# Five norms between FFN, mixer and FFN: roots between GpSimd's pieces, last FFN tiles bank by bank, the first high part read straight from PSUM

## The chip, the cores and the metric

One core of one Trainium2 chip. The metric is the device time of one execution in microseconds (us); lower is better. TensorE multiplies, VectorE (DVE in the rows), ScalarE (ACT) and GpSimd (POOL) work on vectors, and SyncE's queue (SPq) issues the loads.

## What is computed

Two blocks one after the other on x of 256 tokens by 1024 features, all in float32. The first block has a parallel mixer (attention and retention), a cross-attention and a mixture of 32 experts. The second has two layers, each of this form:

```python
for l in range(DEPTH_2):
    x = _layer_norm(alpha * x + 0.5 * _swiglu(x, ffn_w_gu[l, 0], ffn_w_down[l, 0]), ln_g[l, 0], ln_b[l, 0])
    mix = _token_mixers(x, w_in[l], ...)
    x = _layer_norm(alpha * x + mix, ln_g[l, 1], ln_b[l, 1])
    x = _layer_norm(alpha * x + 0.5 * _swiglu(x, ffn_w_gu[l, 1], ffn_w_down[l, 1]), ln_g[l, 2], ln_b[l, 2])
```

`_swiglu(h)` is `(silu(h @ gate) * (h @ up)) @ down` with 2816 hidden features. `_layer_norm` subtracts the mean over the features, divides by the root of the variance, scales and shifts. `_token_mixers` projects x to 2208 columns, mixes the tokens in four ways and projects back.

## The kernel before, in words

Each engine runs one stream of instructions written out by hand, and semaphores order them between engines. Every matrix product is made of three: each float32 operand is split into a high part (rounded by writing it as fp32r) and a low part (the difference), and high x high, high x low and low x high are added in PSUM. ScalarE makes the weights' high parts (`act_high`, L512, and `ffn_high`, L928), VectorE or GpSimd the low ones (`low`, L521, and `ffn_low`, L933; GpSimd in four pieces of 512 columns).

An FFN (`pe_ffn`) goes over 22 tiles of 128 hidden features. `up` puts the gate and up columns of a tile into bank 4 or 5, ScalarE takes the silu (L1106), VectorE multiplies and splits the result (L1158 to L1162: `hf`, `hh`, `hl`), and `down` adds the tile's 1024 output columns for 256 tokens into banks 0 to 3 (tokens 0 to 127 in banks 0 and 1, the others in 2 and 3). `up` of a tile stands before `down` of the tile before it. After tile 21's `up` the last two tiles go bank by bank: tile 20 into banks 0, 1, 2 (nine products), then tile 21 into banks 0, 1, 2, with a semaphore (`f_bk`) behind each, then both into bank 3.

A norm then goes like this; there are six, here called norm 0 to norm 5, after FFN 0, the mixer and FFN 1 of layer 0, and the same of layer 1. `norm_sums` on VectorE adds each bank to x (L1188), takes its statistics (L1189), and after both banks of a token half joins them (L1192), negates the mean (L1194, first half alone) and writes the variance (L1196). GpSimd takes the root (`inverse_root`, L566). ScalarE multiplies mean and root (L1214) and scales the first half of x (L1215); VectorE scales the second half (L1208). TensorE (`pe_norm_T`) first runs 12 products of zeros (L1958), transposes the first half into banks 4 to 7 (L1010, eight), then runs four products of zeros (L1958, or L991 where they also clear banks 0 to 3) and transposes the second half. ScalarE applies gain and bias out of PSUM to `xf` (L1223, two row blocks of 128 features to a bank), VectorE casts that to the high part (`top`, L1235) and subtracts (`rest`, L1239). Before norms 0, 2 and 3 GpSimd has pieces to do: `low` of the projection's chunk 0 and 1 ahead of the roots of norms 0 and 3, `pool_second` (the second tile's low part, L939) ahead of the roots of norm 2. Its pieces for norms 1 and 4 come as late, and stay as they are.

After norms 1, 2 and 4 comes an FFN, whose first tile (`up_first`, L1050) takes all high row blocks first and the low ones after, gate columns (m = 0) before up columns (m = 1), into bank 4:

```python
for low_x in (False, True):
    for m in range(2):
        for k in range(KD):
            if m == 0 and k % 2 == 0: ...wait for the pair of row blocks...
```

After norms 0 and 3 comes the projection (`pe_part`, L1771) in nine chunks of weights, the first of them split in the same way. Between chunks VectorE does other work of the mixer: behind chunk 5's low part `squares()`, behind chunk 6's low part `scales()` (L1454 to L1466), which waits for a root of 16 columns from GpSimd.

In the first block TensorE issues the scores of the attention heads two at a time (`AHEAD1`, `pe_units`), between the retention's products (L2110).

Of the kernel before, what the change touches and what calls it, by code (L numbers as in the profile page):

```python
# [19 lines left out]
ALU = mybir.AluOpType  # L20
# [76 lines left out]
def build(nc, d_x, d_mem, d_w1, d_we, d_wf, d_w2, d_cT1, d_row1, d_wr, d_cT2, d_row2, d_ln, d_tab, d_bias, d_out):  # L97
    ctx = ExitStack()
    with ctx:
# [217 lines left out]
        xp_ok = sem("xp_ok")  # L317
        pre_ok = sem("pre_ok")
# [91 lines left out]
        AHEAD1 = {0: (0, 1), 1: (2, 3), 3: (4, 5), 5: (6, 7)}  # L410
# [103 lines left out]
        def low(eng, run, c, step=None):  # L514
# [4 lines left out]
            for c0 in range(0, n, step):  # L519
                part = slice(c0, c0 + step)  # L520
                ins = eng.tensor_tensor(slot_r[s][:, part], slot[s][:, part], run.highs[c % 2][:, part].bitcast(F32),  # L521
                                        ALU.subtract)
# [413 lines left out]
        def ffn_low_pieces(eng, t, p, done):  # L936

            for c0 in range(0, 2 * D, 512):
                ins = eng.tensor_tensor(wlu[p][:, c0:c0 + 512], ring[:, ring_tile(t) + c0:ring_tile(t) + c0 + 512],  # L939
                                        whu[p][:, c0:c0 + 512].bitcast(F32), ALU.subtract)  # L940
            ins.then_inc(done, 1)
# [21 lines left out]
        def pool_second(pool, g):  # L963
            pool.wait_ge(wl_ok, (g + 1) * FFN_W + 1)
            pool.wait_ge(wh_ok, g * FFN_W + 2)
            ffn_low_pieces(pool, 1, 1, pre_ok)
# [21 lines left out]

        def clear_sums(pe):
# [25 lines left out]
        def pe_ffn(pe, l, f):  # L1015
# [19 lines left out]
            def up_first():  # L1035

                pe.wait_ge(wl_ok, g * FFN_W + FFN_W + 1)
                if g == 0:
                    pe.wait_ge(t_out, tb + 1)
                for low_x in (False, True):  # L1040
                    for m in range(2):
                        for k in range(KD):
                            if m == 0 and k % 2 == 0:
                                if low_x:
                                    pe.wait_ge(t_out, tb + (k // 2 + 1))
                                else:
                                    pe.wait_ge(xh_ok, xb + (k // 2 + 1))
                            cols = slice(k * 2 * P + m * P, k * 2 * P + (m + 1) * P)
                            for w, v in (((whu, xl),) if low_x else ((whu, xh), (wlu, xh))):
                                ins = pe.matmul(bank[4][:, m * S:(m + 1) * S], w[0][:, cols], v[:, k],  # L1050
                                                start=(not low_x and m == 0 and k == 0 and w is whu), stop=False,
# [25 lines left out]
            with pe.Fori(0, FT // 2 - 1) as i:  # L1077
# [1688 lines left out]
```

## Time and profile before

| | |
|---|---|
| median of 3 runs | 1827.29 us (1823.26 to 1829.07) |
| the profiled execution, its own time | 1831.82 us |
| its span, first to last instruction | 1830.0 us |
| TensorE busy | 1645.0 us (90%), VectorE 853.7, ScalarE 639.8, GpSimd 262.6 |
| expert stage, loads at 407 to 427 GB/s | about 320 to 730 us |
| FFN 0, norm 0, mixer, norm 1, FFN 1, norm 2 | 731 to 1278 us |
| the same of layer 1, and norm 5 | 1278 to 1830 us |

TensorE's busy time counts matmuls that overlap, so 90% leaves idle time between stages only. In a tile of an FFN TensorE is never idle (one tile takes 8.55 us); what idle time there is in the second block stands at the norms, in the projection and among the mixer's heads.

### The profile page before, as it was taken

How to read it: one execution, taken by the hardware profiler on the slowest of the kernel's cores; microseconds unless marked ns; L12 is line 12 of the kernel's file. 1: busy time of each engine (PE TensorE's matmuls, PEld its weight loads, DVE VectorE, ACT ScalarE, POOL GpSimd, SP SyncE). 2: the span in 40 equal slices, each digit the busy share in tenths (PEclk: the TensorE clock that was granted, in tenths of full speed). 3: DMA queues.
4: the chain of work that ended last, by engine and by line, in shares of the span. 5: the costliest groups of instructions: out<-in, count | busy, mean ns of one | idle time of the engine just before them, and what ended most of it. 6: DMA issues, size and time to landing. Idle time of an engine off the chain costs nothing.

```text
span 1830.0 us, 29586 instructions
## 1 busy us (share of the span) xinstructions
PE 1645.0 (90%) x11837; PEld 1310.8 (72%) x11837; DVE 853.7 (47%) x1290; ACT 639.8 (35%) x948; POOL 262.6 (14%) x253
## 2 busy tenths in 40 slices
PE   8989999777766776999999899999999999899997
PEld 6777885333323332999977779998999977779996
DVE  4574443111110111555555655555655565666555
ACT  5445442100010011333433644444333333644442
POOL 1233210000000000100143422001300143431000
PEclk9989999977788887999999999999999999999999
DMA  9514578999999999945533054536454543055501
GB/s 393 171 38 138 195 283 334 425 426 427 426 426 426 425 426 407 358 176 188 198 138 138 24 198 180 185 124 236 176 194 180 187 149 124 24 207 182 196 35 46
DMA packets 60949, 421.38 MB, mean 230 GB/s; under 512 B 7008, under 2 KB 16064, under 8 KB 17216
## 3 DMA queue, kind: packets, MB, share of 16 engines
q1 hardware_dynamic: 59136, 409.13, 57.0%
q10 hardware_dynamic: 1728, 11.03, 1.7%
q8 instruction: 64, 1.05, 0.2%
q14 instruction: 21, 0.17, 0.0%
HBM read 419.08 MB, written 1.05 MB: 230 GB/s over the span
## 4 chain that ended last, share of the span: by engine, by line
PE 63%; DMA 10%; SPq 9%; DVE 5%; ACT 5%; POOL 4%; issue 4%; DVEq 0%; ACTq 0%; POOLq 0%
PE bank L1031 26%; PE bank L1072 12%; SPq L1683 9%; PE bank L1820 6%; PE bank L1771 5%; DMA ring<-in_we 4%; DMA more<-in_we 4%; PE bank L1846 2%; PE bank L650 2%; DMA ring<-in_wf 1%; PE bank L1984 1%; POOL small L566 1%; PE bank L1050 1%; PE bank L1965 1%; POOL wlu L939 1%
## 5 line engine op out<-in xcount | busy, mean ns | idle before, releaser
L1031 PE MATMUL bank<-xh,wlu 128*128 128x256 f32 x1344 | 379.9, 283 | 0.0
L1031 PE MATMUL bank<-xh,whu 128*128 128x256 f32 x1344 | 379.8, 283 | 0.0
L1031 PE MATMUL bank<-xl,whu 128*128 128x256 f32 x1344 | 379.8, 283 | 0.0
L1031 PEld LDWEIGHTS bank<-xh,whu 128*128 128x128 f32 x1344 | 257.0, 191 | 3.3
L1031 PEld LDWEIGHTS bank<-xl,whu 128*128 128x128 f32 x1344 | 256.9, 191 | 3.3
L1031 PEld LDWEIGHTS bank<-xh,wlu 128*128 128x128 f32 x1344 | 257.2, 191 | 0.0
L933 DVE TENSOR_TENSOR wlu<-ring,whu 128x2048 fp32r<-128x2048 f32 x84 | 196.3, 2337 | 51.2 <-ACT whu L928 51.2
L933 DVE TENSOR_TENSOR wld<-ring,whd 128x1024 fp32r<-128x1024 f32 x88 | 110.0, 1250 | 188.6 <-ACT whd L928 188.6
L928 ACT ACTIVATE whu<-ring 128x2048 fp32r (+1 forms) x88 | 167.2, 1902 | 3.5 <-DMA ring<-in_wf 3.5
L928 ACT ACTIVATE whd<-ring 128x1024 fp32r (+1 forms) x88 | 93.3, 1060 | 206.1 <-PE bank L1072 202.6
L650 PE MATMUL bank<-ring,xg 128*32 128x256 f32 x1424 | 104.0, 430 | 40.6 <-DMA ring<-in_we 40.6
L1820 PE MATMUL bank<-ring_r,xTh 128*128 128x512 f32 x384 | 112.9, 407 | 9.9 <-POOL ring_r L490 6.0
L1106 ACT ACTIVATE sg<-bank 128x256 f32<-128x256 f32 x88 | 33.8, 384 | 228.5 <-PE bank L1031 210.0
L939 POOL TENSOR_TENSOR wlu<-ring,whu 128x512 fp32r<-128x512 f32 x16 | 20.1, 1287 | 648.8 <-ACT whu L928 614.3
L650 PEld LDWEIGHTS bank<-ring,xg 128*32 128x32 f32 x1424 | 43.9, 119 | 96.1 <-DMA ring<-in_we 68.6
L669 PE MATMUL bank<-ring,hTe 128*32 128x256 f32 x832 | 75.6, 499 | 36.0 <-DMA ring<-in_we 27.6
L829 DVE TENSOR_TENSOR hmid<-hact,bank 128x128 f32<-128x128 f32 x32 | 9.2, 288 | 199.9 <-ACT hact L717 199.9
L1072 PE MATMUL bank<-whd,hl 128*128 128x512 f32 x320 | 100.9, 397 | 0.0
L1072 PE MATMUL bank<-whd,hh 128*128 128x512 f32 x320 | 100.5, 395 | 0.0
L1072 PE MATMUL bank<-wld,hh 128*128 128x512 f32 x320 | 100.4, 394 | 0.0
L1820 PEld LDWEIGHTS bank<-ring_r,xTh 128*128 128x128 f32 x384 | 73.5, 194 | 28.7 <-issue 8.8
L521 POOL TENSOR_TENSOR ring_r<-ring,high 128x512 fp32r<-128x512 f32 x32 | 41.3, 1322 | 349.2 <-ACT high L512 349.0
(317 smaller groups left out, 2745.6 us busy)
## 6 DMA issues: line engine op xcount, KB each, us to landing
ring<-in_we SPq DMA_DIRECT2D x141, 1024.0 KB, 26.8
ring<-in_wf SPq DMA_DIRECT2D x88, 1536.0 KB, 6.8
ring<-in_w SPq DMA_DIRECT2D x52, 1024.0 KB, 4.9
more<-in_we SPq DMA_DIRECT2D x51, 1024.0 KB, 25.7
ring<-in_w SPq DMA_DIRECT2D x32, 256.0 KB, 3.4
ln<-in_ln ACTq DMA_DIRECT2D x6, 1024.0 KB, 4.9
bias<-in_bias ACTq DMA_DIRECT2D x2, 2048.0 KB, 8.1
bias<-in_bias SPq DMA_DIRECT2D x1, 2048.0 KB, 20.1
```

Source lines behind the costliest of these rows:

```text
L521: ins = eng.tensor_tensor(slot_r[s][:, part], slot[s][:, part], run.highs[c % 2][:, part].bitcast(F32), ALU.subtract)
L650: ins = pe.matmul(bank[4 + e % 2][q * CAP:(q + 1) * CAP, 0:2 * P], xg[:, k, e * CAP:(e + 1) * CAP], w[:, kk, q], start=(k == 0), stop=(k = ...
L669: ins = pe.matmul(bank[6][q * CAP:(q + 1) * CAP, 0:2 * P], hTe[:, e % 2, k * CAP:(k + 1) * CAP], w[:, kk, q], start=(k == 0), stop=(k == 3 ...
L928: act.activation(dst[:], ring[:, bass.ds(ring_tile(t) + first, D if down else 2 * D)], ACT.Copy).then_inc(wh_ok, 1)
L933: eng.tensor_tensor(dst[:], ring[:, bass.ds(ring_tile(t) + first, D if down else 2 * D)], src[:].bitcast(F32), ALU.subtract).then_inc(done, 1)
L939: ins = eng.tensor_tensor(wlu[p][:, c0:c0 + 512], ring[:, ring_tile(t) + c0:ring_tile(t) + c0 + 512], whu[p][:, c0:c0 + 512].bitcast(F32), ...
L1031: ins = pe.matmul(bank[4 + p][:, m * S:(m + 1) * S], w[p][:, cols], v[:, k], start=(k == 0 and n == 0), stop=(k == KD - 1 and n == 2))
L1072: ins = pe.matmul(bank[2 * i + c][:], v[p][:, tok(i)], w[p][:, c * 512:(c + 1) * 512], start=False, stop=False, skip_group_check=True)
L1683: sp.dma_start(slot[s], src).then_inc(e_land[s], 16)
L1771: ins = pe.matmul(bank[sel + 2 * i + c0 // 512][:, 0:c1 - c0], v[:, k, tok(i)], w[:, kk, c0:c1], start=(k == 0 and m == 0), stop=(k == KD ...
L1820: ins = pe.matmul(bank[banks[2 * i + h]][:], v[:, k, tok(i)], w[:, kk, h * 512:(h + 1) * 512], start=(k == 0 and m == 0), stop=(k == KD - ...
L1846: ins = pe.matmul(bank[b][:, i * MD:(i + 1) * MD], v[:, k, tok(i)], w[:, k], start=(k == 0 and m == 0), stop=(k == KD - 1 and m == 2))
```

## The change

It has six parts. (1) Norms 0 and 3: the first root stands between the second and third piece of chunk 1's low part; norm 2: between the third and fourth piece of the second tile's. TensorE's second wait in `pe_norm_T` is for the variance, not the root, and the negation of the mean goes from VectorE to ScalarE. (2) The last FFN tiles: tile 20 goes into banks 0 and 1, then tile 21 into bank 0 (both products with `hh` first, that with `hl` last), then tile 20 into bank 2, and the rest as before. (3) The first pair of row blocks: VectorE makes the high part itself out of PSUM, one row block at a time with a semaphore each (`xk_ok`, `xh_ok`), and ScalarE takes that pair last (FFNs) or second (projection). (4) `up_first` goes row block by row block, gate and up columns together, into bank 3, which is cleared with one product of zeros ahead of tile 0's `down`; the low row blocks come in the order in which they are ready; the first pair of tiles is written out ahead of the loops. (5) `scales()` stands behind chunk 7's low part. (6) The heads' scores are issued one at a time from the third on.

```diff
-        AHEAD1 = {0: (0, 1), 1: (2, 3), 3: (4, 5), 5: (6, 7)}
+        AHEAD1 = {0: (0, 1), **{u: (u + 1,) for u in range(1, AH - 1)}}
...
+        ROWS_FIRST = (1, 2, 0, 3)
+
+        def gate_bank(t, p):
+
+            return bank[3 if isinstance(t, int) and t == 0 else 4 + p]
...
                     if i == 1 and b == 0:
-                        pe.wait_ge(pow_ok, POW1 + j // 3 * POW2 + (2, 6, 8)[j % 3])
+                        pe.wait_ge(var_ok, j // 3 * VAR2 + VAR1 + (2, 6, 8)[j % 3])
...
                 for low_x in (False, True):
-                    for m in range(2):
-                        for k in range(KD):
...
+                    order = ROWS_FIRST if low_x and g > 0 else range(4)
+                    for n, k in enumerate(2 * q + h for q in order for h in range(2)):
+                        if low_x and n % 2 == 0:
+                            pe.wait_ge(t_out, tb + (n // 2 + 1))
+                        elif not low_x and k == 0 and g > 0:
+                            pe.wait_ge(xk_ok, l * 3 + (0 if f == 0 else 2))
+                        elif not low_x and (k == 1 or k % 2 == 0):
+                            pe.wait_ge(xh_ok, xb + (k // 2 + 1))
+                        for m in range(2):
...
             up_first()
-            with pe.Fori(0, FT // 2 - 1) as i:
+            up(1, 1)
+            down_ready(0)
+            pe.matmul(bank[3][:], zeros[:, 0:P], zeros[:], start=True, stop=False, skip_group_check=True)
+            down(0, 0)
+            up(2, 0)
+            down(1, 1)
+            with pe.Fori(1, FT // 2 - 1) as i:
...
-            for b in range(3):
-                down_into(FT - 2, 0, b)
-            down_ready(FT - 1)
-            for b in range(3):
+            down_into(FT - 2, 0, 0)
+            down_into(FT - 2, 0, 1)
+            pe.wait_ge(wl_ok, (FT - 1) * 2 + (g * FFN_W + FFN_W + 2))
+            pe.wait_ge(f_hv, (FT - 1) * 2 + (g * FT * 2 + 2))
+            for w in (whd, wld):
+                pe.matmul(bank[0][:], hh[1][:, tok(0)], w[1][:, 0:512], start=False, stop=False, skip_group_check=True)
+            pe.wait_ge(f_h, FT - 1 + (g * FT + 1))
+            pe.matmul(bank[0][:], hl[1][:, tok(0)], whd[1][:, 0:512], start=False, stop=False, skip_group_check=True)\
+              .then_inc(f_bk, 1)
+            down_into(FT - 2, 0, 2)
+            for b in (1, 2):
                 down_into(FT - 1, 1, b, f_bk)
...
-                    if i == 0:
-                        st.then(dve.tensor_scalar(nmean, mean[:, 0, 0:1], -1.0, None, ALU.mult))
-                        st.sync()
...
         def act_norm(act, st, j):
 
+            act.wait_ge(var_ok, j // 3 * VAR2 + VAR1 + (1, 5, 7)[j % 3])
+            st.link(act.activation(nmean, mean[:, 0, 0:1], ACT.Copy, scale=-1.0))
             act.wait_ge(pow_ok, norm_pow(j))
...
+            def first_pair():
+                dve.wait_ge(t_ps, tb + 1)
+                for k, done in ((0, xk_ok), (1, xh_ok)):
+                    dve.tensor_scalar(high[:, k], bank[4][:, k * S:(k + 1) * S], gcol[:, j, 0, k:k + 1],
+                                      gcol[:, j, 1, k:k + 1], ALU.mult, ALU.add).then_inc(done, 1)
...
+            first_pair()
+            top(1)
             if paired:
-                for q in range(4):
+                rest(0)
+                rest(1)
+                for q in (2, 3):
                     top(q)
                     rest(q)
             else:
-                for q in range(4):
-                    top(q)
-                for q in range(4):
-                    rest(q)
+                rest(1)
+                top(2)
+                rest(2)
+                top(3)
+                rest(0)
+                rest(3)
...
-                    if c == 6:
+                    if c == 7:
                         scales()
...
+                low(pool, run2(l, 0), 0, 512)
+                low(pool, run2(l, 0), 1, 512, lambda c0: root(1, 0) if c0 == CH // 2 else None)
+                root(1, 1)
...
-                    pool_second(pool, g + 1)
-                for i in range(NT):
-                    pool.wait_ge(var_ok, l * VAR2 + (VAR1 + 7 + i))
-                    inverse_root(pool, rs[:, i:i + 1])
+                    pool_second(pool, g + 1, lambda c0: root(7, 0) if c0 == 3 * CH // 4 else None)
+                else:
+                    root(7, 0)
+                root(7, 1)
```

How the order of the instructions moves is seen in three places. GpSimd at norm 0: before, two chunks' pieces (`ring_r`) and then both roots (`small`):

```order
L521 TENSOR_TENSOR ring_r<-ring,high_0_88 128x512 [waits dh_ok]
L521 TENSOR_TENSOR ring_r<-ring,high_0_88 128x512 x3
L521 TENSOR_TENSOR ring_r<-ring,high_1_89 128x512 [waits dh_ok]
L521 TENSOR_TENSOR ring_r<-ring,high_1_89 128x512 x3
L566 TENSOR_TENSOR small<-small,minus_half 128x1 [waits var_ok] x2
```

and in the changed kernel:

```order
L524 TENSOR_TENSOR ring_r<-ring,high_0_88 128x512 [waits dh_ok]
L524 TENSOR_TENSOR ring_r<-ring,high_0_88 128x512 x3
L524 TENSOR_TENSOR ring_r<-ring,high_1_89 128x512 [waits dh_ok]
L524 TENSOR_TENSOR ring_r<-ring,high_1_89 128x512
L569 TENSOR_TENSOR small<-small,minus_half 128x1 [waits var_ok]
L524 TENSOR_TENSOR ring_r<-ring,high_1_89 128x512 x2
L569 TENSOR_TENSOR small<-small,minus_half 128x1 [waits var_ok]
```

The first root has moved ahead of two of the eight pieces. VectorE at norm 0, the tiles being the high part `xTh`, the full value `xf` and the low part `xl`; in the changed kernel this stands there, where before there were four pairs of CAST and TENSOR_TENSOR, one for each pair of row blocks in turn:

```order
L1269 TENSOR_SCALAR xTh_87<-bank,gcol 128x256 [waits t_ps]
L1269 TENSOR_SCALAR xTh_87<-bank,gcol 128x256
L1274 CAST xTh_87<-xf 128x512 [waits xf_ok]
L1280 TENSOR_TENSOR xl<-xf,xTh_87 128x512 [waits xh_ok,xf_ok]
L1280 TENSOR_TENSOR xl<-xf,xTh_87 128x512 [waits xh_ok]
L1274 CAST xTh_87<-xf 128x512 [waits xf_ok]
L1280 TENSOR_TENSOR xl<-xf,xTh_87 128x512 [waits xh_ok]
```

The first two instructions wait for TensorE's transposes alone, no longer for ScalarE. VectorE at the end of the projection, before; `ring_r` is a chunk's low part (6, 7 and 8 here), `proj` the scales:

```order
L521 TENSOR_TENSOR ring_r<-ring,high_0_88 128x2048 [waits dh_ok]
L1454 TENSOR_SCALAR proj_134<-proj_134,small 128x256 [waits pow_ok]
...
L1466 TENSOR_TENSOR proj_134<-proj_134,row_64 128x384 [waits dve_step] x2
L521 TENSOR_TENSOR ring_r<-ring,high_1_89 128x2048 [waits dh_ok]
L521 TENSOR_TENSOR ring_r<-ring,high_0_88 128x1280 [waits dh_ok]
```

In the changed kernel the scales stand between the last two, behind chunk 7:

```order
L1513 TENSOR_TENSOR proj_134<-proj_134,row_64 128x384 [waits dve_step] x2
L524 TENSOR_TENSOR ring_r<-ring,high_0_88 128x1280 [waits dh_ok]
```

So the wait for GpSimd's root (`pow_ok`) has moved behind chunk 7's low part and ahead of chunk 8's.

## Rows read from the trace of the kernel before

**Rows 1.** What TensorE waited for: us in total, times, longest

```profile
PE bank L1771 <- DVE ring_r L521: 4.5, 2, 2.3
```

**Rows 2.** Timeline around norm 0: start, us, engine, line, out<-in, count, idle before

```profile
920.96 5.00 POOL L521 TENSOR_TENSOR ring_r<-ring,high 128x512 fp32r<-128x512 f32 x4 [5.97 <-ACT high L512]
924.09 2.76 PE L1958 MATMUL bank<-zeros 128*128 128x512 bf16 x12
926.83 1.24 ACT L1215 ACTIVATE x<-x,small 128x1024 f32<-128x1024 f32 x1
927.82 0.15 DVE L1196 TENSOR_SCALAR small<-small 128x1 f32<-128x1 f32 x1
928.12 1.09 PE L1010 MATMUL bank<-ident,x 128*128 128x128 f32 x8 [1.26 <-ACT x L1215]
929.91 1.04 PE L1010 MATMUL bank<-ident,x 128*128 128x128 f32 x8
930.39 3.75 ACT L1223 ACTIVATE xf<-bank,gcol 128x256 f32<-128x256 f32 x8 [2.33 <-PE bank L1010]
931.93 0.73 PE L1771 MATMUL bank<-high,xTh 128*128 128x512 f32 x2 [0.98 <-DVE xTh L1235]
```

**Rows 3.** Timeline of the last tiles of FFN 1 and the start of norm 2

```profile
1266.17 0.39 PE L1057 MATMUL bank<-whd,hh 128*128 128x512 f32 x1
1267.57 0.43 DVE L1162 TENSOR_TENSOR hl<-hf,hh 128x256 fp32r<-128x256 f32 x1
1268.74 0.40 PE L1057 MATMUL bank<-wld,hh 128*128 128x512 f32 x1
1269.27 0.69 DVE L1188 SCALAR_TENSOR_TENSOR x<-x,bank 128x512 f32<-128x512 f32 x1 [1.28 <-PE bank L1057]
```

**Rows 4.** Timeline of norm 2, GpSimd, ScalarE and TensorE

```profile
1268.72 5.01 POOL L939 TENSOR_TENSOR wlu<-ring,whu 128x512 fp32r<-128x512 f32 x4 [160.57 <-ACT whu L928]
1271.98 1.06 ACT L928 ACTIVATE whd<-ring 128x1024 fp32r<-128x1024 f32 x1 [3.42 <-PE bank L1057]
1274.27 0.29 ACT L1214 ACTIVATE small<-small 128x1 f32<-128x1 f32 x1 [1.24 <-POOL small L566]
1275.89 1.09 PE L1010 MATMUL bank<-ident,x 128*128 128x128 f32 x8 [1.35 <-ACT x L1215]
```

**Rows 5.** Starts of FFN 1 and FFN 2: timeline of ScalarE and VectorE

```profile
1080.79 3.75 ACT L1223 ACTIVATE xf<-bank,gcol 128x256 f32<-128x256 f32 x8 [2.33 <-PE bank L1010]
1282.29 2.49 DVE L1239 TENSOR_TENSOR xl<-xf,xh 128x512 fp32r<-128x512 f32 x4
```

**Rows 6.** Chain of waits there: start, us, engine, tile, line, count

```profile
1085.06 4.58 PE bank L1050 x36
1281.52 6.75 PE bank L1050 x40
```

**Rows 7.** Timeline of the projection of layer 0

```profile
939.85 3.22 DVE L521 TENSOR_TENSOR ring_r<-ring,high 128x2048 fp32r<-128x2048 f32 x1 [3.67 <-ACT high L512]
965.88 1.92 ACT L512 ACTIVATE high<-ring 128x2048 fp32r<-128x2048 f32 x1 [3.66 <-PE bank L1771]
968.51 0.35 DVE L1454 TENSOR_SCALAR proj<-proj,small 128x256 f32<-128x256 f32 x1 [2.81 <-POOL small L566]
971.56 4.08 DVE L521 TENSOR_TENSOR ring_r<-ring,high 128x2048 fp32r<-128x2048 f32 x2
973.90 0.50 PE L1771 MATMUL bank<-high,xTh 128*128 128x512 f32 x1 [2.27 <-DVE ring_r L521]
```

**Rows 8.** TensorE in stretches: busy (count), granted clock, DMA share, GB/s

```profile
974.00:976.00 2.00, 2.00 (x7) 0.68 0.00 0
976.00:978.00 2.00, 2.00 (x6) 0.50 0.00 0
1282.00:1284.00 2.00, 2.00 (x10) 0.50 0.00 0
```

**Rows 9.** Timeline of VectorE among the first block's heads

```profile
110.39 0.69 DVE L2055 SCALAR_TENSOR_TENSOR lg<-bank,bias 128x512 f32<-128x512 f32 x1 [0.73 <-PE bank L1965]
```

More of the change, by code:

```diff
@@ L512, in act_high, with low @@
             act.activation(run.highs[c % 2][:, 0:n], slot[run.slots[c]][:, 0:n], ACT.Copy).then_inc(dh_ok, 1)
-        def low(eng, run, c, step=None):
+        def low(eng, run, c, step=None, between=None):
             eng.wait_ge(dh_ok, run.high + (c + 1))
@@ L1101, in act_ffn, with tiles @@
             else:
-                act_norm_T(act, l * 3 + (f - 1 if f == 0 else 1), tb)
+                act_norm_T(act, l * 3 + (f - 1 if f == 0 else 1), tb, (1, 2, 3, 0))
             def silu(t, p):
                 act.wait_ge(f_gu, t + (g * FT + 1))
-                act.activation(sg[:, p], bank[4 + p][:, 0:S], ACT.Silu).then_inc(f_sg, 1)
+                act.activation(sg[:, p], gate_bank(t, p)[:, 0:S], ACT.Silu).then_inc(f_sg, 1)
             def down_free(t):
                 act.wait_ge(f_dn, t + (g * (FT + 1) + 1))
-            with act.Fori(0, FT // 2 - 1) as i:
+            def tiles(i):
                 for p in range(2):
@@ L1117, in act_ffn @@
                     ffn_high(act, g, i * 2 + (p + 2), p, False)
+            tiles(0)
+            with act.Fori(1, FT // 2 - 1) as i:
+                tiles(i)
             j = l * 3 + 2 * f
@@ L1162, in hidden, with tiles @@
                 dve.tensor_tensor(hl[p][:], hf[:, p], hh[p][:].bitcast(F32), ALU.subtract).then_inc(f_h, 1)
-            with dve.Fori(0, FT // 2 - 1) as i:
+            def tiles(i):
                 for p in range(2):
@@ L1168, in dve_ffn @@
                     low(i * 2 + (p + 2), p, False)
+            tiles(0)
+            with dve.Fori(1, FT // 2 - 1) as i:
+                tiles(i)
             hidden(FT - 2, 0)
@@ L1215, in act_norm, with act_norm_T @@
             act.activation(x[:, 0], x[:, 0], ACT.Identity, bias=nmr, scale=rs[:, 0:1]).then_inc(x0_ok, 1)
[L1217 removed]
+        def act_norm_T(act, j, tb, order):
             act.wait_ge(gcol_ok, 1)
[L1220 to L1226 removed]
@@ L1228, in dve_norm_T @@
-        def dve_norm_T(dve, j, high, paired=False):
+            for q in order:
+                act.wait_ge(t_ps, tb + (q + 1))
+                if q == 0:
+                    act.wait_ge(xh_ok, j * 4 + 5)
+                for k in (2 * q, 2 * q + 1):
+                    ins = act.activation(xf[:, k], bank[4 + q][:, (k % 2) * S:(k % 2 + 1) * S], ACT.Identity,
+                                         bias=gcol[:, j, 1, k:k + 1], scale=gcol[:, j, 0, k:k + 1])
+                ins.then_inc(xf_ok, 1)
@@ L1577, in pool_layers, with root @@
                     pool_affine(pool, st, l * 3 - 1, (wl_ok, (g + 1) * FFN_W + 4))
-                for c in range(2):
-                    low(pool, run2(l, 0), c, 512)
-                for i in range(NT):
-                    pool.wait_ge(var_ok, l * VAR2 + (VAR1 + 1 + i))
+                def root(n, i):
+                    pool.wait_ge(var_ok, l * VAR2 + (VAR1 + n + i))
                     inverse_root(pool, rs[:, i:i + 1])
+                low(pool, run2(l, 0), 0, 512)
+                low(pool, run2(l, 0), 1, 512, lambda c0: root(1, 0) if c0 == CH // 2 else None)
+                root(1, 1)
                 pool_affine(pool, st, l * 3, (t_out, tb + 4))
@@ L1780, in pe_part @@
                         for kk in range(per):
+                            if kk == 1 and passes == (0, 1):
+                                pe.wait_ge(xh_ok, tops)
                             for i in range(NT):
```

47 lines of the change are left out of this document (20 added, 27 removed).

## The prediction

> **What bounds the kernel now.** I read the page first: TensorE is busy for nine tenths of the span, the other engines for half of it or less, and outside the expert stage, which this change does not touch, the loads keep up. So the second block's time is TensorE's, and the change can only win where TensorE idles or runs slowly. The list of its waits comes next [rows 1]: two waits of 2.3 us for a chunk's low part in the projection, one a layer. The rest stands around the norms, which I read in the timelines of norm 0 [rows 2], of the last tiles of FFN 1 [rows 3] and of norm 2 [rows 4]; the two halves of x are found there at the end of a chain sums, root, scaling, transposes, and TensorE waits for it. Behind a norm the FFN's first tile waits for VectorE's high parts [rows 5], and the chain of waits shows what it costs: the last 36 of its products take 4.58 us at full clock, but 40 take 6.75 us in FFN 2 [rows 6], where the granted clock stood at 0.50 [rows 8]. All sums below are made against the profiled execution, 1831.82 us by its own time; the median of the runs, 1827.29, is 4.5 us lower, and I take the same saving off it.
>
> **(a) Last tiles.** From the product at 1266.17 to the last at 1268.74 there are 11 steps of 0.233 us [rows 3]. Bank 0 was complete after 12 products, it now is after 9: 0.70 us earlier. Bank 1 stays at product 15, which holds the gain of VectorE's sums to 0.65, no more. The low part `hl`, ready at 1268.00 [rows 3], is wanted by the ninth product at about that time, so no stall comes in. The negation of the mean leaves VectorE, about 0.18 us with its step (an instruction of that size is 0.15, as L1196 in [rows 2]). Statistics come 0.83 us earlier. This counts in full only in norm 5, where nothing but the norm is left to do: **-0.8**. In norms 1 and 4 the roots come as before, so nothing changes there.
>
> **(b) Norms 0 and 3.** GpSimd works on the second of two chunks until 925.96, 920.96 + 5.00 [rows 2]; only then comes the root, and ScalarE scales from 926.83 to 928.07. Now the root stands before the last two of the four pieces, 2.5 us sooner, so after 923.46; the variance is there at 924.1 (by (a)), the root by 924.7, ScalarE is done about 926.3. That is earlier than TensorE is: its 12 products of zeros run from 924.09 for 2.6 us, to 926.7. So transposes begin at 926.7 for 928.12, **-1.4**, and the second half follows: four products of zeros end at 928.6 and the second half of x, whose root also stands 0.8 earlier, is ready by 928.3. The two pieces that moved behind the root feed chunk 1, wanted later than 927.2, when they end. Then the first pair: before, ScalarE starts `xf` at 930.39 and the first product runs at 931.93, 1.6 us after the transposes [rows 2]. Now VectorE writes one row block's high part straight from PSUM. No row of before shows this operation on 256 columns; from below half of the 512 columns out of PSUM (0.69, L1188 in [rows 3]) gives 0.35, from above all of it, 0.69; I take 0.43, what `hl` takes for 256 columns [rows 3], since the shape is the same. With 0.1 for the semaphore the first product comes 0.53 us behind the transposes for 1.6: **-1.07**. Together -2.5 a layer, **-5.0** (bounds -4.3 to -5.3). The work of the other pairs is the same, reordered; the low parts that start the third pass are 1.4 us earlier than wanted.
>
> **(c) The scales.** VectorE waits 2.81 us for GpSimd's root of 16 columns before it can start `scales` at 968.51, and then still has its work to do, so chunk 7's low part starts at 971.56 though its high part ended at 967.80 (965.88 + 1.92), and TensorE idles 2.27 us to 973.90 [rows 7]. Now VectorE starts it at 967.8. It takes about 2.35 (971.56 to 973.90), so it is there by 970.2, and TensorE wants it at 971.6: the stall goes, **-2.4 a layer, -4.9**. What is queued behind: the scales run from 970.2 to 973.3, chunk 8's low part (4.08 less 2.35, so 1.73) to 975.0, and TensorE, at 5.5 us a chunk (ScalarE's casts follow its chunks 3.66 + 1.92 = 5.6 apart, [rows 7]), wants it at 977.1. That leaves 2 us. The root itself is ready at 968.5 and no longer waited for.
>
> By [rows 7] another low part of 2048 columns took 3.22 us, while GpSimd was scaling; the 2.35 above had it idle. The Trainium skill ("SBUF — State Buffer", Who interferes with whom) says that VectorE and GpSimd share a port pair under an exclusive lock, the loser blocked for the whole instruction. This trace agrees in kind. By the page the worst is one GpSimd instruction, a piece of 1.25 us, met once by chunk 7 or the first pair; chunk 7 has a margin of 1.4, so the sum would be the same.
>
> **(d) The clock behind that stall.** Behind the idle stretch the granted clock is 0.68 and 0.50 for two stretches of 2 us [rows 8]. At full clock the same work would need 1.36 and 1.0: 1.6 us lost, and layer 1 shows the same. If the idle time goes, nothing lets the clock fall there; I take 1.5 each, **-3.0** (bounds 0 and -3.3).
>
> **(e) Starts of the FFNs behind norms 1, 2 and 4.** A is the time when ScalarE starts `xf`, 1080.79 in FFN 1 [rows 5]. The first tile ended at 1085.06 + 4.58 = 1089.64 [rows 6], A + 8.85, the last high pair having started at A + 4.27 with gate and up (m = 0, then all of m = 1) behind it. Now all eight products of a pair come together, and only eight of the high pass are left for the last pair. ScalarE leaves out the first pair, so the last pair is cast one pair sooner (two times 0.47 of 3.75 / 8), at A + 2.8 for its input, A + 3.9 with the cast and what stands on VectorE before it, a low part of 0.62 (2.49 / 4) [rows 5]. Eight products at 0.127 (4.58 / 36) to A + 4.9, sixteen low ones to A + 6.9: **-2.0 each, -6.1**. VectorE has about 0.2 us to spare here before tile 1; if it hasn't, each gives 1.0 only (-3).
>
> **(f) Norm 2.** GpSimd's four pieces take 5.01 us from 1268.72 [rows 4]; the root now comes after three, at 1272.5. But ScalarE casts `whd` to 1273.04 first, then has the negation (as L1214, 0.29), product and scaling to do (1.24): x is ready at 1274.9 where transposes began at 1275.89, **-1.0**.
>
> **(g)** The FFN 2 start: 40 products in 6.75 us would take 5.1 at the pitch of FFN 1; 36 against 36, 1.3 us come from the clock [rows 6, 8]. With less idle time ahead it should not fall: **-1.3** (bounds 0 and -1.6).
>
> **(h)** One product of zeros more an FFN, 0.22 (2.76 / 12, [rows 2]), four times: **+0.9**. In FFN 0 nothing is gained, for its operands are ready early.
>
> **(i) The heads.** From the third on scores come one at a time, so fewer of them stand ahead of VectorE's first logits, for which it waited 0.73 [rows 9]: **-0.8** (bounds -1.5 and +1, if a single score ahead is too little and VectorE waits among the heads).
>
> Sum: -0.8 - 5.0 - 4.9 - 3.0 - 6.1 - 1.0 - 1.3 + 0.9 - 0.8 = -22.0. The profiled time would be 1809.8, the median **1805** (1827.29 - 22.0 = 1805.3).
>
> **The rivals.** *Clock* (0.19): (d) and (g), 4.3 us, come not from the idle time but fall elsewhere, and as many again may be found: 1809.6 to 1813.9. For it speaks that 0.50 is granted after some stalls and not after others. The Trainium skill ("TensorE: Matmul & The Clock Gate", Part 1) has a gate that follows recent activity on a grid of its own, so that a dip can shift in time as work shifts; the sum by it would hold the 4.3 us back, 1809.6. The dips I read stand only behind idle stretches [rows 8], which is why I hold to the sum.
>
> *The stall moves* (0.08): the root of 16 columns or the scales are late, chunk 8 waits as chunk 7 did: (c) and (d) lost, 7.9 us, 1813. It decides if scales end over 2 us later than reckoned.
>
> *The feed* (inside the range): FFN starts give 1.0 each and no more, 1808.5.
>
> *Little happens* (0.04): the chain at the norms has another link, as the products of zeros behind the norms or VectorE's casts, and each gain waits there: above 1822.
>
> *Slower* (0.03): the first pair of tiles is written out ahead of the loop in each FFN on three engines, so TensorE's stream grows by some hundreds of instructions, which must be fetched. If fetching them stalled TensorE by over 22.0 / 4 = 5.5 us an FFN, the sum turns: at 7 us an FFN the time is 1805.3 + 28 = 1833. Against it: the 36 products of [rows 6] are written out as well and run at 0.127 without a gap.
>
> **How the numbers follow.** The sum as it stands has 0.66. Its own bounds (b 0.7, e 3, i 1.8 up; 1.0 or so down, and a stronger gain in dips elsewhere, 4) give about 1799 to 1810; with the clock rival the range goes up to 1814, and down to 1797, beyond which less than 2 in 10 is left. A measurement can tell 0.3%, 5.5 us. Faster by more than that: 0.66 + 0.19 + 0.08 less a remainder, 0.92; same 0.05; slower 0.03.
>
> **What would show it.** In the changed kernel's profile: the wait of 2.3 us for `ring_r` absent from TensorE's waits, the clock at 1.00 behind it; chunk 8 without a wait; the transposes of norm 0 about 1.4 us earlier after the last product, set by the products of zeros; VectorE's first high part about 0.43 us; FFN 1's first tile ending about 6.9 us after its transposes; the last bank sums of the end 0.8 us nearer to the last product. Wrong is the prediction if TensorE's idle time has shrunk and the time hasn't (the clock), or if a first tile's end is at A + 8 or more (VectorE).

## The result, and the profile after

The changed kernel's median is **1806.27 us** (12 runs, 1800.8 to 1821.08), that of the kernel before 1827.72 (12 runs, 1821.37 to 1832.12): ratio 0.9887, 95% interval 0.9869 to 0.9904, so 1.0 to 1.3% faster. The forecast was 1805.

The page of the changed kernel, against a span of 1830.0 and TensorE at 1645.0 us before:

```profile
span 1805.4 us, 29475 instructions
PE 1645.2 (91%) x11841; PEld 1305.3 (72%) x11841; DVE 856.1 (47%) x1289; ACT 617.6 (34%) x935; POOL 258.8 (14%) x253
```

TensorE is as long busy as before: what went is time in which it waited. Its waits between 930 and 1060 us (us in total, times, longest), the stretch that holds the projection and the mixer of layer 0:

```profile
PE bank L2035 <- ACT xT L2091: 4.1, 7, 0.8
PE bank L2026 <- ACT lg L2085: 1.4, 4, 0.5
```

The wait for `ring_r` of [rows 1] is absent, as is its clock stretch [rows 8] at that place. The projection's end in the timeline (start, us, engine, line, out<-in, count, idle before):

```profile
958.76 1.92 ACT L513 ACTIVATE high<-ring 128x2048 fp32r<-128x2048 f32 x1 [3.66 <-PE bank L1820]
960.72 2.29 DVE L524 TENSOR_TENSOR ring_r<-ring,high 128x2048 fp32r<-128x2048 f32 x1 [2.12 <-ACT high L513]
962.92 0.35 DVE L1501 TENSOR_SCALAR proj<-proj,small 128x256 f32<-128x256 f32 x1
965.97 1.49 DVE L524 TENSOR_TENSOR ring_r<-ring,high 128x1280 fp32r<-128x1280 f32 x1
```

Chunk 7's low part now starts 0.04 after its high part; before it was 3.8 later [rows 7]. The scales find their root ready and end at 965.9, and chunk 8's low part at 967.5 keeps nobody waiting.

Norm 0 in the timeline, to be read beside [rows 2]:

```profile
919.51 2.76 PE L2009 MATMUL bank<-zeros 128*128 128x512 bf16 x12
919.52 0.56 POOL L569 TENSOR_TENSOR small<-small,minus_half 128x1 f32<-128x1 f32 x1 [0.83 <-DVE small L1226]
920.50 1.24 ACT L1247 ACTIVATE x<-x,small 128x1024 f32<-128x1024 f32 x1
922.11 1.04 PE L1021 MATMUL bank<-ident,x 128*128 128x128 f32 x8
924.27 0.99 DVE L1269 TENSOR_SCALAR xTh<-bank,gcol 128x256 fp32r<-128x256 f32 x2
924.55 1.93 ACT L1257 ACTIVATE xf<-bank,gcol 128x256 f32<-128x256 f32 x4 [2.81 <-PE bank L1021]
924.87 0.73 PE L1820 MATMUL bank<-high,xTh 128*128 128x512 f32 x2
```

The root stands at 919.5, in front of two of GpSimd's pieces; ScalarE is done at 921.74, 0.37 ahead of the transposes, which start as the products of zeros end (twelve at 0.22 behind 919.51). VectorE's high part of one row block out of PSUM takes 0.50 (0.99 for two), and the first product comes 0.60 behind VectorE's start.

The first tiles of FFN 1 and FFN 2, in the chain of waits (start, us, engine, tile, line, count), to be read beside [rows 6]:

```profile
1070.22 6.39 PE bank L1061 x48
1265.06 6.39 PE bank L1061 x48
```

In both FFNs the 48 products follow each other at 0.13. Before, FFN 2's last 40 alone took 6.75.

The new order of the last tiles has a price of its own. The last product of tile 20 into bank 1 and the first ones of tile 21 into bank 0, at the end of FFN 0:

```profile
914.87 0.40 PE L1069 MATMUL bank<-wld,hh 128*128 128x512 f32 x1
915.22 0.47 PE L1106 MATMUL bank<-whd,hh 128*128 128x512 f32 x1
915.52 0.40 PE L1106 MATMUL bank<-wld,hh 128*128 128x512 f32 x1
```

The steps are 0.35 and 0.30 where all others are 0.23. So from the last `hl` to the last product of an FFN it is 4.17 us for 3.97 before, in all four FFNs, and 3.97 again in the run with the old order (experiment 8): the order costs 0.2 an FFN. Why the two steps are longer is not shown.

**A ledger by stretches.** The starts of single instructions serve as marks in every profile: the first silu of each FFN, and ScalarE's casts of the chunks of weights (a stretch "FFN" ends at the cast of the next projection's chunk 0, a stretch "rest of the projection, mixer" at the last cast before the next FFN). How much shorter a stretch is than in the first profile of before (its length there in brackets) tells what each part did, however the whole run fell out. The last two columns are the same programs, profiled once more in the runs `after_again` and `before_again` below.

| stretch | changed | changed, again | before, again |
|---|---|---|---|
| start to first silu of FFN 0 (742.00) | -5.01 | -6.75 | -4.52 |
| FFN 0 (165.3) | +0.23 | +0.23 | +0.01 |
| norm 0, to cast of chunk 2 (30.64) | -2.28 | -2.29 | 0.00 |
| rest of the projection, mixer, layer 0 (126.91) | -4.21 | -6.95 | +0.03 |
| norm 1, start of FFN 1 (24.87) | -1.77 | -1.79 | +0.02 |
| FFN 1, norm 2, start of FFN 2 (198.62) | -3.76 | -3.76 | -0.09 |
| norm 3 (30.62) | -2.27 | -2.27 | 0.00 |
| rest of the projection, mixer, layer 1 (126.90) | -3.55 | -3.60 | +0.05 |
| norm 4, start of FFN 3 (24.87) | -1.79 | -1.79 | +0.02 |
| norm 5, last `hl` to the first scaling of x (8.04) | -0.70 | -0.71 | 0.00 |

FFNs 2 and 3 give +0.2 each, as FFN 0. Every stretch repeats within 0.1 us, but for the first block and the two with a mixer.

What the clock takes is reckoned in all that follows as (one less the granted clock) times the time. From the cast of chunk 8 to the end of a mixer's stretch the kernel before loses 5.1 us a layer in this way, in all six mixers seen (its two profiles and that of `heads_alone`, whose second block is the same): 1.7 behind the stall [rows 8], and 3.4 at the mixer's end. That second dip was not among the rows of before. Here it is in layer 0 (length, TensorE's busy time and count, granted clock, DMA share, GB/s):

```profile
1046.00:1048.00 2.00, 1.41 (x9) 0.60 0.03 8
1048.00:1050.00 2.00, 2.00 (x12) 0.50 0.94 291
1050.00:1052.00 2.00, 2.00 (x9) 0.50 0.57 238
1052.00:1054.00 2.00, 2.00 (x8) 0.69 0.00 0
```

### The profile page after: what moved, and what is told of

Read it like the earlier page. It is cut to its first block, busy times and chain, and to the rows that moved or that the text cites. A ratio compares the mean times of both kernels' runs of the same rounds, so it can differ in the third digit from the quotient of the medians.

```text
span 1805.4 us, 29475 instructions
## 1 busy us (share of the span) xinstructions
PE 1645.2 (91%) x11841; PEld 1305.3 (72%) x11841; DVE 856.1 (47%) x1289; ACT 617.6 (34%) x935; POOL 258.8 (14%) x253
## 4 chain that ended last, share of the span: by engine, by line
PE 66%; DMA 11%; SPq 10%; issue 4%; ACT 3%; DVE 3%; POOL 3%; DVEq 0%; ACTq 0%; POOLq 0%
PE bank L1042 27%; PE bank L1084 12%; SPq L1732 10%; DMA ring<-in_we 9%; PE bank L1820 7%; PE bank L1871 6%; PE bank L1897 2%; DMA ring<-in_wf 1%; PE bank L2035 1%; PE bank L1061 1%; PE bank L653 1%; PE bank L2016 1%; PE bank L2009 1%; PE bank L1069 1%; POOL ring_r L491 1%
## 5 line engine op out<-in xcount | busy, mean ns | idle before, releaser
L931 ACT ACTIVATE whd<-ring 128x1024 fp32r (+1 forms) x88 | 93.2, 1060 | 206.8 <-PE bank L1084 203.2
L653 PE MATMUL bank<-ring,xg 128*32 128x256 f32 x1424 | 111.7, 454 | 37.8 <-DMA ring<-in_we 37.8
```

What stands on the lines that cost most here:

```text
L653: ins = pe.matmul(bank[4 + e % 2][q * CAP:(q + 1) * CAP, 0:2 * P], xg[:, k, e * CAP:(e + 1) * CAP], w[:, kk, q], start=(k == 0), stop=(k = ...
L931: act.activation(dst[:], ring[:, bass.ds(ring_tile(t) + first, D if down else 2 * D)], ACT.Copy).then_inc(wh_ok, 1)
```

## The experiments

There are twelve runs: the changed kernel and the one before once more each, and ten kernels that differ from one of the two. Where a kernel ran several times, its median stands beside that of before, taken at the same time.

**1. The changed kernel once more** (`after_again`).

> The changed kernel once more, for one more profile. If the ledger of stages is a property of the program, the stages of the second block repeat within 0.3 us each: norm 0 -2.3, projection with what follows it -4.1, FFN 1 start -1.8, norm 2 with FFN 2 start -3.8 against the first profile of before. If instead the granted clock falls by chance, the stretches at 0.5 and 0.7 stand elsewhere and the stages differ by 1 to 3 us. The first block's gain of 5.8 us, of which I had forecast 0.8, should be seen in either case; if it shrinks to about 1, it was chance.

1802.55 us (one run). The ledger above: norms and FFN starts repeat to 0.02 us. The mixer of layer 0 does not: it is 2.7 us shorter, where the first profile had the clock at 0.50 to 0.70 from 1034 to 1042 us, at the end of the heads and behind it, and this one at 1.00.

**2. The scales behind chunk 6 again** (`scales_behind_6`).

```diff
-                    if c == 7:
+                    if c == 6:
                         scales()
```

> The change with the scales back behind chunk 6's low part, nothing else undone. My theory (c and d together): TensorE waits 2.3 us for ring_r in each layer, and the clock is at 0.5 to 0.7 behind it; in all 3.9 a layer, so 7.8 us slower than the changed kernel, 1814. Rival: the clock has nothing to do with that stall; then 4.9 slower, 1811, and the granted clock is 1.00 behind the stall or falls in other stretches.

1813.75 us (6 runs, before 1829.28; ratio 0.9927, 0.9906 to 0.9948), 7.5 above the changed kernel where the theory said 7.8 and the rival 4.9. The intervals of the two ratios leave some 2 to 12 us for this difference, so the medians don't choose between the two. The stall is back in both layers, but the clock behind it is not the same in both. The timeline's row of the stall in layer 0, then TensorE's stretches (length, busy and count, granted clock, DMA share, GB/s), two behind that stall and three behind that of layer 1:

```profile
965.81 0.50 PE L1820 MATMUL bank<-high,xTh 128*128 128x512 f32 x1 [2.28 <-DVE ring_r L524]
```

```profile
966.00:968.00 2.00, 2.00 (x9) 1.00 0.00 0
968.00:970.00 2.00, 2.00 (x10) 1.00 0.00 0
1503.00:1505.00 2.00, 1.72 (x6) 0.84 0.00 0
1505.00:1507.00 2.00, 2.00 (x6) 0.50 0.00 0
1507.00:1509.00 2.00, 2.00 (x9) 0.81 0.03 8
```

The same stall, and in layer 0 no dip behind it. So the fall to 0.50 is not a fixed price of the stall, though close to it: it stands behind seven of the eight such stalls in the profiles, and in none of the 20 mixers without the stall is there a fall at that place. Stretch of the mixer in the ledger: -1.53 and +0.54, for -3.55 to -6.95 in the changed kernel.

**3. The scales moved, nothing else** (`scales_behind_7_alone`, on the kernel before).

> The kernel before with only the scales moved behind chunk 7's low part. Theory: the stall of 2.3 us and the clock stretch behind it go, 3.9 a layer in the ledger from chunk 8's cast to the mixer's end, 7.8 in all, 1821 for 1828.5. Against it: the seven profiles with the stall gone show stretches at granted clock 0.50 among the heads that cost 0, 0, 0.5, 1.1, 2.0, 3.4 and twice 8.0 us by execution, so the median may give 2 to 3 us less (1824) and the runs spread wider than before's.

1820.15 us (6 runs, 1815.45 to 1823.8; before 1829.23; ratio 0.995, 0.9932 to 0.9968), 9.1 less by the medians. In the ledger -2.70 and -2.68 in the mixers, where 2.3 is the stall: in this profile the clock takes 5.1 us a layer from the cast of chunk 8 on, as much as in before; the fall behind the stall is gone, and another one has come in among the last heads.

This run shows something else. FFN 1, norm 2 and the start of FFN 2 are 1.25 shorter here, though none of their instructions were changed: the granted clock, 0.50 at FFN 2's start in the three profiles of before and `heads_alone` [rows 8], is 1.00 there in this one. That is the whole of (g), without any idle time taken away.

**4. The heads of the first block** (`heads_in_pairs` on the changed kernel, `heads_alone` on the kernel before).

```diff
-        AHEAD1 = {0: (0, 1), **{u: (u + 1,) for u in range(1, AH - 1)}}
+        AHEAD1 = {0: (0, 1), 1: (2, 3), 3: (4, 5), 5: (6, 7)}
```

> The change with the first block's scores two at a time again, nothing else undone. By my forecast 0.8 us slower, 1807. By the trace of the changed kernel, where the heads end 3.5 us earlier and the first block 5.8 us earlier, 3 to 6 us slower, about 1811, with a stretch at granted clock 0.5 among the heads (110 to 150 us) as in before.

> The kernel before with only the first block's scores one at a time. By my forecast 0.8 us faster than before; by the trace of the changed kernel 3 to 6 us faster, 1822 to 1824, with TensorE's granted clock at 1.00 from 110 to 150 us. If it is no faster, the first block's gain belongs to where the work fell, not to this part.

In pairs on the changed kernel: 1810.68 us (6 runs; before 1829.28; ratio 0.9909, 0.9886 to 0.9932), 4.4 above, with overlapping intervals. Alone on before: 1826.51 (12 runs; ratio 0.9988, 0.9972 to 1.0004), no difference that can be told. The profiles say more: from the first score to the end of the heads it takes 42.3 to 42.9 us singly (eight profiles), 44.8, 45.0, 45.0 and 46.5 in pairs (four), and 49.7 and 51.5 singly in the other two (experiments 8 and 9). Most of that is clock, which takes 1.7 us there in each of the eight, 3.4 to 5.1 in the pairs, and 10.2 and 12.0 in the two; what is left is 40.6 to 41.2 in the eight and 39.7 to 41.6 in pairs. In those two the clock falls and stays. Stretches of `last_tiles_as_before`, whose first block is the changed kernel's:

```profile
104.00:110.00 6.00, 6.00 (x21) 0.50 0.00 0
110.00:120.00 10.00, 10.00 (x39) 0.50 0.01 2
120.00:130.00 10.00, 9.54 (x60) 0.92 0.00 0
```

**5. The kernel before once more** (`before_again`).

> The kernel before once more, for a second profile. The ledger of the changed kernel's two profiles and of the one with the heads in pairs starts the second block 4.5 to 6.7 us earlier than the first profile of before, though the pairs have the first block of before word for word. My theory now: the first profile of before lost about 4 us there to stretches of a lower granted clock, by chance; so this one starts its second block 3 to 5 us earlier than that one (first tile of FFN 0 done at 737 to 739 for 742.0), and its stages behind that repeat within 0.3 us, but for one stretch among the heads of a layer. Rival: before is slow there for a reason in the program, and repeats 742.0 within 1.

1827.31 us. Its first silu comes 4.52 us earlier, everything behind it in step within 0.1 us a stretch. So the profiled execution of before was slow by 4.5 us in its first block alone, of which 1.5 lay between the first score and the end of the heads; that is the whole distance of its time to the median. Counted from this second profile, the single scores bring FFN 0's first silu 0.5 to 3.3 us earlier in eight profiles, and 3.1 and 9.9 later in the two above.

**6. The roots behind the pieces again** (`roots_behind_pieces`).

```diff
-                low(pool, run2(l, 0), 1, 512, lambda c0: root(1, 0) if c0 == CH // 2 else None)
+                low(pool, run2(l, 0), 1, 512, None)
+                root(1, 0)
...
-                    pool_second(pool, g + 1, lambda c0: root(7, 0) if c0 == 3 * CH // 4 else None)
+                    pool_second(pool, g + 1, None)
+                    root(7, 0)
```

> The change with both roots behind GpSimd's pieces again (norms 0, 2 and 3). Theory: the transposes of norms 0 and 3 wait for the scaled x as before, 1.4 us each, and norm 2 gives 1.0 back: 3.8 us in all; in the ledger norm 0 gains 0.9 for 2.3 and norm 2 with its FFN start 2.8 for 3.8. Rival: VectorE's statistics and the products of zeros set the end, and the roots' place gives under 0.5 each.

1817.28 us (one run). Norm 0 gains 0.94 for 2.28, norm 3 0.91 for 2.27, norm 2 with its start 2.77 for 3.76: 3.7 us, as expected. ScalarE waits for the root again, and TensorE for ScalarE:

```profile
921.17 1.24 ACT L1247 ACTIVATE x<-x,small 128x1024 f32<-128x1024 f32 x1
922.46 1.09 PE L1021 MATMUL bank<-ident,x 128*128 128x128 f32 x8 [1.13 <-ACT x L1247]
```

The other 7 us of this run lie in the mixers, -2.41 and +2.05, with the clock at 0.50 for 10 us on end in layer 1 and twice more behind that (7.8 us lost to the end of the heads).

**7. The first pair through `xf`, and gate before up** (`first_pair_through_xf`, `gate_before_up`). The first lets ScalarE take the pairs in order and VectorE cast:

```diff
-            for q in order:
+            for q in range(4):
                 act.wait_ge(t_ps, tb + (q + 1))
...
-                dve.wait_ge(t_ps, tb + 1)
+                dve.wait_ge(xf_ok, j * 4 + 1)
                 for k, done in ((0, xk_ok), (1, xh_ok)):
-                    dve.tensor_scalar(high[:, k], bank[4][:, k * S:(k + 1) * S], gcol[:, j, 0, k:k + 1],
-                                      gcol[:, j, 1, k:k + 1], ALU.mult, ALU.add).then_inc(done, 1)
+                    dve.tensor_copy(high[:, k], xf[:, k]).then_inc(done, 1)
```

The second puts `for m in range(2)` of `up_first` outside the row blocks, the waits on m == 0.

> The change with the first pair's high part made from xf again (ScalarE takes the pairs in order 0 to 3, VectorE casts row block by row block). Theory: the projection starts 1.1 us later behind norms 0 and 3 (ledger 1.2 for 2.3), and the FFNs' last pair comes 0.5 to 0.6 later behind norms 1, 2 and 4 (1.2 for 1.8): 3.8 us in all. Rival: TensorE is held by the last pair's high part in the projection too, and the first pair's start is worth under 0.5.

> The change with the first tile's gate products ahead of its up products again, within the high and the low pass. Theory: 36 products instead of 24 are left behind the last pair's high part, 12 more at 0.12: the first tile of FFNs 1, 2 and 3 ends 1.4 us later, 4.3 us in all (ledger 0.4 for 1.8). Rival: the feed of low parts holds the end, and it gives under 0.7 each.

1812.3 and 1812.27 us (one run each). The first pair: norms 0 and 3 gain 1.43 and 1.40, so it is worth 0.85 and 0.87 there; FFN starts 1.06, 3.05 and 1.03, so 0.7 each; 3.9 in all. Gate before up: FFN starts 0.33, 2.35 and 0.36, so 1.4 each, 4.3 in all. Both sums are as expected to 0.1 us; of the first the parts are less so, for the projection's start was put at 1.1 and the FFN's at 0.5 to 0.6. In the first of them the clock fell in the mixer of layer 0 and stayed down for 10 us while TensorE's records leave no gap. Just before, it had waited 0.78 for ScalarE:

```profile
1003.57 1.08 PE L2032 MATMUL bank<-proj,xT 128*128 128x64 f32 x8 [0.78 <-ACT xT L2088]
```

```profile
1004.00:1006.00 2.00, 1.96 (x17) 1.00 0.00 0
1006.00:1008.00 2.00, 2.00 (x12) 0.51 0.00 0
1008.00:1010.00 2.00, 2.00 (x11) 0.50 0.00 0
1010.00:1012.00 2.00, 2.00 (x11) 0.50 0.02 4
```

**8. The last tiles in their old order** (`last_tiles_as_before`).

```diff
+            for b in range(3):
+                down_into(FT - 2, 0, b)
+            down_ready(FT - 1)
+            for b in range(3):
+                down_into(FT - 1, 1, b, f_bk)
```

These lines stand in place of the changed kernel's.

> The change with the last two tiles' products in the order of before (tile 20 into banks 0, 1, 2, then tile 21), nothing else undone. Theory: bank 0 is complete 0.7 us later, so the statistics start later and norm 5 takes 0.65 more; norms 0 and 3 lose less, for the products of zeros set their end (x was ready 0.3 before they ended), about 0.3 each; norm 2 loses 0 to 0.5. In all 1.3 to 1.8. Rival: all of the 0.7 in norm 5 came from the removed negation, and the order gives nothing.

1816.28 us (one run, with the long clock stretch of the first block shown above). Norm 5 gives 0.20 for 0.70, so the order is worth 0.50 and the negation, by subtraction, 0.20; norms 0 and 3 lose 0.48 and 0.50, norm 2 0.1 or less: 1.5 in all. I had 0.3 for norms 0 and 3. In norm 0 the first half's transposes come 0.36 later behind FFN 0's last product, for x is no longer ready before the products of zeros end; the second half's come 0.25 later still and the first product of the projection another 0.05; and the last product itself comes 0.2 earlier, the price of the new order given back.

**9. Single scores in the second block too** (`mixer_scores_singly`).

```diff
+        AHEAD2 = {0: (0, 1), **{u: (u + 1,) for u in range(1, 19)}}
```

> The change with the second block's scores one head at a time too (from the third on), as the change does in the first block. Theory: TensorE's waits of 0.3 to 0.8 us for ScalarE at every second head are filled by the scores that now come there, the heads end 2 to 4 us a layer earlier, and with less idle time the granted clock falls there less often: 1798 to 1802, and a narrower spread. Rival: the chain softmax, transpose, copy of one head sets the pitch, whatever TensorE does between; then the same within 2 us, or slower by up to 4 where a score is late for VectorE.

1812.74 us (5 runs, 1811.78 to 1825.89; before 1829.23; ratio 0.9913, 0.9895 to 0.993): slower than the change by 6.5 by the medians, by 4.8 by the ratios, whose intervals just touch. Faster it is not, and the ledger is clearer than the runs. Two heads' scores of `after_again`, then one head's of this kernel:

```profile
992.42 1.13 PE L2016 MATMUL bank<-qkT 32*128 32x256 f32 x8
```

```profile
995.62 1.12 PE L2015 MATMUL bank<-qkT 32*128 32x256 f32 x4
```

Eight products for two heads take what four take for one, for two heads lie in different rows of the array. The Trainium skill ("TensorE: Matmul & The Clock Gate", Part 3: Packing small matmuls) says that products in different row groups run at the same time; these rows agree. Issued singly, each second head costs 1.1 us more, and the waits that it fills are 0.3 to 0.8. Layer 0's mixer is 3.5 us longer here than in the change's first profile (-0.66 for -4.21 in the ledger), and in both the clock takes 3.4 of it: that is what the single scores cost a layer. In layer 1 the clock stood at 0.50 for some 20 us (10 lost) with TensorE busy throughout, and before it fell TensorE had been idle for 0.3 us in 10:

```profile
1540.00:1550.00 10.00, 9.71 (x66) 1.00 0.00 0
1550.00:1571.00 21.00, 21.00 (x81) 0.51 0.00 1
```

**10. Products of zeros in the waits among the heads** (`zeros_in_gaps`).

```diff
-        MIX_KEEP = [(0, 6)] + [(0, 0)] * 19
+        MIX_KEEP = [(0, 6)] + [(u % 2, 0) for u in range(1, 18)] + [(2, 0)] * 2
```

> The change with products of zeros in the waits among the second block's heads: one of 128 rows by 512 columns ahead of the values of every second head, where TensorE waited 0.34 to 0.78 us for ScalarE, and two ahead of the last two (0.78 each); 11 a layer at 0.22 each. Theory: they lie in waits and cost 0 to 1 us; and since they keep TensorE busy with full rows, the stretches at granted clock 0.50 among the heads (0 to 8 us lost by layer and execution) become rarer: median 1801 to 1805, spread narrower than the change's 1800.8 to 1821.1. Rival: what sets those stretches lies elsewhere in the heads, in the small tiles themselves, and the time is the change's or 1 us above it, 1806 to 1808, with 0.50 among the heads in its profile as often.

**1800.87 us** (5 runs, 1799.0 to 1801.48; before 1831.03; ratio 0.9839, 0.9817 to 0.9861). It beats both kernels: its interval (just) lies below the change's, and its five runs lie within 2.5 us where the change's twelve span 20. Its one profile starts FFN 0 1.1 us earlier than the best of the change, by its first block, which is the change's. The clock in layer 0's mixer, and two of the added products:

```profile
961.00:981.00 20.00, 19.55 (x133) 1.00 0.47 165
981.00:1001.00 20.00, 18.93 (x127) 1.00 0.01 1
1001.00:1021.00 20.00, 19.18 (x143) 1.00 0.00 1
1021.00:1033.00 12.00, 10.76 (x74) 1.00 0.00 1
```

```profile
1030.95 0.60 PE L2009 MATMUL bank<-zeros 128*128 128x512 bf16 x2
1031.80 1.11 PE L2035 MATMUL bank<-vm,xT 128*128 128x64 f32 x8 [0.25 <-ACT xT L2091]
```

Of the 0.78 that TensorE waited here 0.25 is left. In the ledger the mixers give -6.82 and -6.22, against -6.95 for the change at its best, so the zeros themselves (13 a layer, not the 11 I had counted) cost 0.1 to 0.7 a layer, and in this profile the granted clock is 1.00 from the last cast of the projection to the end of the heads in both layers.

## Why the prediction was right, and where it was not

The forecast of 22.0 us stands against 21.5 by the medians. So close a fit is in part luck. In the ledger, with the mixers' mean, all terms but (i) come to 18.7, where 21.2 were forecast; the rest is the size of what the first block gives in most profiles (0.5 to 3.3), of which only 0.8 had been forecast. By its own steps:

- **(a)** -0.8: measured -0.70 in norm 5 (0.50 the order, 0.20 the negation). That no stall comes in was nearly so: the new order costs TensorE 0.2 an FFN, which counts in norms 0, 2 and 3 and stood in no term.
- **(b)** -2.5 a layer: -2.28. The 12 products of zeros set the end, as reckoned (0.37 us of slack for x). Behind the last product of FFN 0 the projection's first product comes 2.47 earlier: 1.42 at the first transposes, 0.05 at the second ones, and 1.00 behind them for 1.07, since VectorE's high part took 0.50 for 0.43. What is missing from the sum is the 0.2 of the new order.
- **(c)** the stall, put at 2.4 where the row has 2.27: gone in both layers, and chunk 8 waits for nothing. The rival of the late scales is out.
- **(d)** -1.5 a layer for the clock: right about the place, too narrow about the cause. I held that the idle time caused the dip and that without it the clock had no reason to fall. At that place it did not fall again. But the larger dip of before, 3.4 us at the mixer's end, stands behind waits of 0.8 and none of the parts touches it, and other dips come and go among the heads. From the cast of chunk 8 on, the eight profiles without the stall (all but those of experiments 9 and 10) lose 0 us in three of their 16 mixers, 3.4 in seven, 5.1 in four and 10.2 in two: 4.05 in the mean for the 5.1 of before. In the ledger these 16 range from -7.01 to +2.05, mean -3.4 and median -3.55, for a forecast of -3.9 with (c). Less the stall, that leaves 1.1 in the mean and 1.3 in the median for (d). This is the clock rival, to which I gave 0.19: its mechanism is real, its size in the median was small, and it is why the change's runs spread over 20 us.
- **(e)** -2.0 a start (its own terms add to 1.95): -1.8. From ScalarE's start (A) to the end of the tile it is 6.8 as reckoned, but A itself is 0.2 later: ScalarE now begins with the second pair, which TensorE has transposed one pair later. VectorE's thin margin ahead of tile 1 held: the feed rival is out.
- **(f), (g)** norm 2 and FFN 2: -1.0, -2.0 and -1.3, with the 0.2 of (h) in between, made 4.1 together; measured -3.76, short by the two times 0.2 under (a) and (e). The cause given for (g) does not hold, though: experiment 3 has the clock at 1.00 there with norm 2 as before, and experiment 6 has it with the roots' idle time put back. So the 1.25 us came with the change, but not from the shorter wait; what moved the dip is not shown.
- **(h)** +0.2 an FFN: +0.21 to +0.23. Writing out the first pair of tiles cost nothing else, so the slower rival is out.
- **(i)** -0.8 was argued from one wait of 0.73. The typical profile gains 0.5 to 3.3 before FFN 0, but in two of ten it loses 3 to 10 to the clock, and the runs (12 alone, 6 undone) don't settle the sign of the mean. What I missed is that single scores use TensorE worse, four products taking what eight took, and that what the profiles do gain there is mostly clock.
- My basis, the profiled execution 4.5 us above the median, was sound by luck: those 4.5 us lay in the first block, where no term but (i) was read.

What stays open is what the chip counts when it lets the clock fall among small products. Experiment 10 has two mixers without a dip in its one profile, and five runs close together, so full products in the waits seem to end it; whether it is their rows, their columns or the shorter gaps wasn't separated. That a given dip merely shifts, because the work ahead of it did, was not tested by itself either, and experiment 3 speaks for it at FFN 2's start. How large (d) is in the mean isn't settled within 2 us.

## What to carry to other kernels

Read what an edit gives from marks in the trace, stretch by stretch, before reading it from the whole time: here nearly all parts repeated to 0.1 us while single runs of one program differed by up to 20. List all dips of the clock before crediting one to a stall: the largest of the second block stood unread at the mixers' ends. Where TensorE works on small products with short waits between, its clock is the largest unknown of the sum, whether a nearby stall is removed or not; a few products of zeros in waits that exist anyway bought 5 us and a narrow spread. And before splitting a group of small products, look whether they run side by side.

## What the runs showed of the hardware that was not expected

- TensorE's granted clock fell to 0.50 (1.2 GHz) and stayed there for 10 to 20 us while its records show it 100% busy, mostly with products of 32 to 128 rows by 64 to 256 columns (experiments 4, 7 and 9); in the same code of other executions, or of the other layer, it stood at 1.00. Waits of TensorE stood before most falls, 0.78 us in experiment 7 and 1.48 in 4, but before the one of experiment 9 no more than 0.3 in 10 us. The Trainium skill ("TensorE: Matmul & The Clock Gate", Part 1) names idle gaps as the cause of a fall; the fall of experiment 9 came with hardly a gap before it, and the long stretches at 0.50 had none in them.
- Eight score products of two heads took 1.13 us (`after_again`), four of one head 1.12 (`mixer_scores_singly`).
- VectorE's scaling of 256 columns out of PSUM took 0.50 us a row block (changed kernel, norm 0); the cast of 256 columns from SBUF 0.25 (0.49 for two, `first_pair_through_xf`).
